# Second block's mixers in one stream of equal steps: every product with hT taken from weights in two parts, eight ring slots lent, gates by tanh

## The reference

```
for l in range(DEPTH):                                    # DEPTH = 2
    x = x + 0.5 * swiglu_ffn(x, ffn1_norm[l], ffn1_wi[l], ffn1_wo[l])
    h = rms_norm_2(x, mix_norm[l])
    (sb_q, sb_k, sb_v, mla_cq, mla_ckv, mla_kr, nsa_q, ck, cv, sk, sv, wk, wv,
     nsa_gate, merge_gate) = jnp.split(h @ w_in[l], offsets, axis=-1)
    o_sb = stick_breaking_attention(sb_q, sb_k, sb_v)     # 8 heads of 64
    o_mla = mla_attention(mla_cq, mla_ckv, mla_kr, ...)   # 8 heads, 64 + 32 wide
    o_nsa = nsa_attention(nsa_q, ck, cv, sk, sv, wk, wv, nsa_gate, ...)
    gates = sigmoid(merge_gate).reshape(B, S, 3, D_MODEL)
    y = gates[:, :, 0] * (o_sb @ proj_sb[l]) + gates[:, :, 1] * (o_mla @ proj_mla[l]) \
        + gates[:, :, 2] * (o_nsa @ proj_nsa[l])
    x = x + y @ w_out[l]
    x = x + 0.5 * swiglu_ffn(x, ffn2_norm[l], ffn2_wi[l], ffn2_wo[l])
```

## Time and profile before

| | us |
|---|---|
| median of 3 runs | 2982.14 |
| the profiled execution | 2984.02 |
| its span | 2982.7 |
| first mixer, norm to w_out's end | about 1566 to 1964 |
| second mixer, the same | about 2372 to 2779 |
| the four feed-forwards | about 202 to 212 each |

### The profile page before, as it was taken

One profiled execution on the slowest core, in us unless ns is written; L12 is line 12 of the kernel. 1 busy time (PEld: TensorE's weight loads), 2 busy tenths in 40 slices (PEclk: granted clock), 3 DMA queues, 4 the chain that ended last, 5 costly groups with the idle time before them and its releaser, 6 DMA issues.

```text
span 2982.7 us, 31836 instructions
## 1 busy us (share of the span) xinstructions
PE 2459.9 (82%) x13622; PEld 1558.7 (52%) x13622; DVE 1093.7 (37%) x1874; ACT 800.0 (27%) x1143; POOL 3.2 (0%) x7
## 2 busy tenths in 40 slices
PE   7877656767877766677999888889999898887999
PEld 5542111113552111116988454579889774545897
DVE  3741000003640000005544435555455543446554
ACT  3230000002520000004433322444344433324443
POOL 0000000000000000000000000000000000000000
PEclk9888899888878888888999898999999998999999
DMA  8769999997459999998653233356655432424562
GB/s 316 256 233 409 409 409 409 409 409 296 155 224 409 409 409 409 409 409 230 183 184 113 58 92 109 124 141 184 186 155 183 156 112 71 142 71 127 149 180 95
DMA packets 397106, 703.68 MB, mean 236 GB/s; under 512 B 17187, under 2 KB 232483, under 8 KB 396838
## 3 DMA queue, kind: packets, MB, share of 16 engines
q1 hardware_dynamic: 396966, 701.65, 66.2%
HBM read 700.56 MB, written 1.05 MB: 235 GB/s over the span
## 4 chain that ended last, share of the span: by engine, by line
PE 59%; DMA 24%; DVE 7%; ACT 4%; SPq 4%; issue 1%; DVEq 0%; ACTq 0%
PE psum L696 57%; DMA ring<-in_moe_w_up 8%; DMA ring<-in_moe_w_gate 8%; DMA ring<-in_moe_w_down 8%; SPq L566 4%; PE psum L700 2%; DVE arena L1833 1%; ACT ring L1396 1%; DVE lent_r L1833 1%; ACT lent_r L1396 1%; DVE arena L1841 1%; DVE arena L1844 1%; DMA ring<-in_ada_w 0%; DMA ring<-in_cmp_wv 0%; DVE arena_r L1833 0%
## 5 line engine op out<-in xcount | busy, mean ns | idle before, releaser
L696 PE MATMUL psum<-ring,arena 128*32 128x512 f32 (+3 forms) x3672 | 685.4, 664 | 287.3 <-DMA ring<-in_moe_w_up 101.8
L696 PE MATMUL psum<-lent_r 128*128 128x256 f32 (+1 forms) x3440 | 637.8, 299 | 14.3 <-DVE lent_r L1833 14.3
L696 PEld LDWEIGHTS psum<-ring,arena 128*32 128x32 f32 (+2 forms) x3672 | 182.7, 129 | 791.7 <-issue 260.3
L696 PEld LDWEIGHTS psum<-lent_r 128*128 128x128 f32 x3440 | 551.6, 195 | 33.9 <-DVE lent_r L1833 12.1
L696 PE MATMUL psum<-arena_r,lent_r 128*128 128x256 f32 (+1 forms) x1888 | 520.4, 317 | 16.5 <-DVE lent_r L1833 9.3
L1833 DVE TENSOR_TENSOR lent_r<-ring,lent_r 128x2048 fp32r<-128x2048 f32 (+1 forms) x158 | 349.3, 2212 | 279.6 <-ACT lent_r L1396 279.5
L696 PEld LDWEIGHTS psum<-arena_r,lent_r 128*128 128x128 f32 x1888 | 368.0, 195 | 40.1 <-DVE lent_r L1833 10.3
L1396 ACT ACTIVATE lent_r<-ring 128x2048 fp32r<-128x2048 f32 (+1 forms) x158 | 289.9, 1839 | 155.2 <-PE psum L696 154.8
L1396 ACT ACTIVATE arena<-psum 128x512 f32<-128x512 f32 (+3 forms) x118 | 57.8, 501 | 1009.5 <-PE psum L696 935.9
L696 PE MATMUL psum<-ring,hT 128*128 128x512 f32 (+1 forms) x576 | 272.3, 609 | 3.8 <-ACT arena L1396 2.8
L696 PE MATMUL psum<-lent_r,arena_r 128*128 128x512 f32 x1056 | 241.6, 390 | 0.3
(11 more groups left out here) (143 smaller groups left out, 1504.0 us busy)
## 6 DMA issues: line engine op xcount, KB each, us to landing
ring<-in_moe_w_gate SPq DMA_DIRECT2D x128, 1024.0 KB, 18.6
ring<-in_moe_w_up SPq DMA_DIRECT2D x128, 1024.0 KB, 18.6
ring<-in_moe_w_down SPq DMA_DIRECT2D x128, 1024.0 KB, 18.7
ring<-in_ffn_wi SPq DMA_DIRECT2D x176, 512.0 KB, 5.1
ring<-in_ada_w SPq DMA_DIRECT2D x48, 1024.0 KB, 7.5
ring<-in_w_in SPq DMA_DIRECT2D x46, 1024.0 KB, 5.1
ring<-in_ffn_wo SPq DMA_DIRECT2D x44, 1024.0 KB, 4.9
ring<-in_w_out SPq DMA_DIRECT2D x8, 1024.0 KB, 4.8
```

The costliest lines, as they stand in the source:

```text
L696: return T.matmul(out, lhsT, rhs, start=start, stop=stop, **kw)
```

## The change

- The plain `hT` is no longer written; its place holds the high part (`hT_r`). All of w_in is cut: the eight groups of `fill_cols` are 16 pieces more, and the NSA gates one of 192 columns. In the mixers the low part is written over the weight in its ring slot (`ring_r`), so the slot is held until its products end (`multiplied`); the high part goes to one of two buffers.
- `lend(MIX_LENT)` lends eight slots, five go round. After w_out's load two come back.
- One generator `main()` on each of PE, ACT and DVE holds 26 pieces (`mi_list`: low, low, f0, f2, sv, sv, f1, f3, f4, gates, 16 fills) in four steps each, and the products of the first two branches with their projections in 16 steps, 120 steps in all. A step on PE is 12 products of 256 columns or 6 of 512. It uses banks 6 and 7 in turn.
- `mixer_start` runs 9 steps, then `mla_prepare` in 5 parts with 6, 3, 3, 2, 2 steps between (MLA_LEAD). A has a step at each turn of a stream, B too, C two (STEPS_C). Before the second half of the compression `far_enough` runs the stream on to step 57, so that keys and values are there.
- MLA's preparation has banks 4 and 5; its seven first copies go from DVE to ACT. NSA attention turns in bank 4 alone and has its output in bank 5.
- The compression's first product has the weight as the stationary operand and gives the turned result; the transpose and DVE's copy after it go.
- sigmoid(z) is 0.5 + 0.5 tanh(z/2): ACT copies the gates out of PSUM with Tanh; DVE's `opened` does (tanh + 1) x product, and the factor 0.5 is in y's parts. Only the third branch is merged after C.

```diff
-STEPS_A = (1, 1, 3)
+MIX_LENT = 8
+SPLIT = (0, 1, 2, 3, 4, 5, 6, 7)
+MLA_LEAD = (6, 3, 3, 2, 2)
+STEPS_A = (1, 1, 2)
-STEPS_C = 1
+STEPS_C = 2
...
+    mi_list = [("low", 0), ("low", 1), ("f", 0), ("f", 2), ("sv", 0), ("sv", 1), ("f", 1), ("f", 3), ("f", 4), ("gates", 0)] + [
+        (n, h) for n in SPLIT for h in range(2)]
...
     def piece(st, c, p, *pieces):
-            load((st, c, p), E.cut_low.at(st, c, p, 1), *pieces)
+            load((st, c, p), multiplied(st, c, p) if st in in_place else E.cut_low.at(st, c, p, 1), *pieces)
...
+            lend(MIX_LENT)
+            for p in range(4):
+                mi(p)
+            load(("uq", layer), ...)
+            mi(4)
+            load(("ukv", layer), ...)
+            for p in range(5, 9):
+                mi(p)
+            piece("mi", layer, mi_list.index(("gates", 0)), cols_chunk(w, C_GATE, 24))
+            fill_loads(layer, 0)
+            fill_loads(layer, 1)
+            compress_loads(layer, 0)
+            fill_loads(layer, 2)
+            compress_loads(layer, 1)
+            for i in range(3, 8):
+                fill_loads(layer, i)
...
+    KV_STEPS = 4 * (mi_list.index((1, 1)) + 1) + 1
+    def mixer_start(fill, mla):
+        for _ in range(9):
+            next(fill)
+        for n in MLA_LEAD:
+            next(mla)
+            for _ in range(n):
+                next(fill)
...
+                for p, (kind, i) in enumerate(mi_list):
+                    T.wait_ge(*E.cut_low.at("mi", l, p, 1 if p else 0))
+                    for j in range(2):
+                        b = 6 + j
...
+                            for k in range(4):
+                                kk = 4 * i + k
...
+                                op = mm3(psum[:, b, 0:width], (high[:, kk, tok], low[:, kk, tok]),
+                                         cut_part("mi", l, p, k * width, width), kk == 0, kk == KT - 1)
+                                if k == 1:
+                                    step()
+                                    yield
...
-            weave(fill, STEPS_C, (attention(nsa_units, 12 + 12 * l, bufs=mx.bufs), 1))
+            weave(fill, STEPS_C, (attention(nsa_units, 12 + 12 * l, turn_banks=(4,), out_bank=5, bufs=mx.bufs), 1))
             run(fill)
-            for br in range(3):
...
+            T.wait_ge(*E.o_low.at(l, 2))
+            for h in range(2):
+                if h:
+                    T.wait_ge(*E.o_low.at(l, 3))
+                rows_piece_product("mo", l, 4 + h, mx.oT_high[2], mx.oT_low[2], 2 * h, 4, [0, 1, 2, 3])
...
+                for p, (kind, i) in enumerate(mi_list):
+                    if p:
+                        second(p - 1)
+                    if p + 1 < n_mi:
+                        cut("mi", l, p + 1)
...
+                    stt(mx.y[:, t, half], mx.merge[:, br, t, half], 1.0, psum[:, bank, :], ALU.add, ALU.mult)
```

More of the change, by code:

```diff
@@ L1793, in mixer @@
-            run(fill)
-            C.preload_act_table(ACT.Sigmoid)
-            cut("mo", l, 0, 0)
-            for br in range(3):
-                if br == 2:
-                    C.wait_ge(*E.o_out.at(12 + 12 * l + 7))
-                af(mx.oT_high[:, br], mx.oT[:, br], ACT.Copy).then_inc(*act.ev(E.o_high, l, br))
-            for br in range(3):
-                af(mx.merge[:, br], mx.merge[:, br], ACT.Sigmoid).then_inc(*act.ev(E.opened, l, br))
-            pieces = cuts("mo", l, 10)
-            for _ in range(6):
-                next(pieces)
+            C.wait_ge(*E.o_out.at(8 + 12 * l + 3))
@@ L1808, in mixer @@
-            run(pieces)
+                af(mx.yT_high[:, k, :], psum[:, 4 + k % 4, 0:S], ACT.Copy, scale=0.5).then_inc(*act.ev(E.yT_high, l, k))
+            cut("mo", l, 8)
+            cut("mo", l, 9)
         C.wait_ge(E.cols_in, 16)
@@ L2497, in mixer, with opened @@
-            for i2, (c0, width) in enumerate(mi_tokens):
-                next(pieces)
-                next(pieces)
-                V.wait_ge(*E.mi_pe.at(l, ("t", 2 * i2 + 1)))
-                dst = (mx.sv, mx.low)[i2][:, 0, :]
-                cp(dst, psum[:, 2 * i2, 0:width]).then_inc(*dve.ev(E.mi_dve, l, ("t", i2)))
+            cut("mi", l, 0, 1)
+            done = [0]
+            def opened(br, b):
+                t, half = b // 2, slice(b % 2 * 512, (b % 2 + 1) * 512)
+                bank = 6 + b % 2 if br < 2 else b
+                V.wait_ge(*E.rows.at("mo", l, 2 * br + 1, b))
+                if br == 0:
+                    stt(mx.y[:, t, half], mx.merge[:, br, t, half], 1.0, psum[:, bank, :], ALU.add, ALU.mult).then_inc(
+                        *dve.ev(E.merged, l, br, b))
+                else:
+                    alone(stt(mx.prod[:, b % 2, :], mx.merge[:, br, t, half], 1.0, psum[:, bank, :], ALU.add, ALU.mult))
+                    tt(mx.y[:, t, half], mx.y[:, t, half], mx.prod[:, b % 2, :], ALU.add).then_inc(*dve.ev(E.merged, l, br, b))
@@ new lines, in mixer @@
+            weave(fill, STEPS_B[0], (attention(mla_units, 8 + 12 * l, [(0, 1)], [2], 3, mx.bufs), STEPS_B[1]), (nsa_all(), STEPS_B[2]))
+            weave(fill, STEPS_C, (attention(nsa_units, 12 + 12 * l, turn_banks=(4,), out_bank=5, bufs=mx.bufs, after=after), 1))
+            run(fill)
+            cut("mo", l, 4)
+            cut("mo", l, 5)
+            o_low(3)
+            for b in range(4):
+                opened(2, b)
+                if b == 1:
+                    cut("mo", l, 6)
+            cut("mo", l, 7)
```

620 lines of the change are left out of this document (357 added, 263 removed).

## The result

The changed kernel takes 3099.07 us (median of 4 runs, 3095.14 to 3099.27) against 2982.76 (2981.45 to 2986.21): a ratio of 1.038, with a 95% interval of 1.037 to 1.040. The forecast was 2902, with a range of 2846 to 2952. The change is slower by 116 us, 58 a mixer. The runs that follow are compared by medians, their stretches by the profiled execution of each.

A forecast was written before the change was run, and what follows sets the result against it. TensorE bound the first products; small waits and low clock added time in stick-breaking (A), MLA (B) and NSA attention (C). Per mixer -6.2 to attention's end, -30.7 after, -3 at the start: -39.9, two -80, 2902 us; range 2846 to 2952.

The forecast's parts named there:

- Fill products: Stick-breaking through NSA attention: plain products taking 132.5 us become products of parts at 88.3, a gain of 44 a mixer.
- Clock: Stick-breaking and MLA attention: of at most 24 us lost to half clock, 5 a mixer are won back.
- The sign that I named for it: Clock forecast is wrong if the granted clock in stick-breaking and MLA attention is below 0.86.
- The ring: Mixers' weight loads: five slots instead of seven add 6 us of TensorE idle time a mixer, range 0 to 16.
- My sign for it: Ring forecast is wrong if TensorE's wait for a DMA at the compression is over 10 us.
- The cuts in the queues: DVE and ACT orders: softmax steps late behind weight cuts cost 3 us a mixer, range 0 to 40.
- Rival 3: Slower: TensorE waits for a 4.2 us cut pair at each of 20 pieces, 84 us a mixer; 3066 us; chance 0.07.
- my own sign, over 1 us a piece: Queue forecast is wrong if TensorE waits for cuts for over 1 us a piece.
- The compression: NSA preparation: keeps its 64 products in other shapes; its transposes and their waits go, -3 us a mixer.
- NSA attention: Summed with stick-breaking and MLA attention as one stretch; 22.1 us of branch products paid in the stream.
- the end: Last attention product to first w_out product: 52.2 us become 21.5, a gain of 30.7 a mixer.
- the waits at the second turn in C: NSA attention, one bank for turning: TensorE waits for ACT about 1.2 us each; 5 us a mixer counted.

The follow-up runs named there:

- e4: Changed kernel with one product instead of three in each fill step, low-part products left out: 3058.6 us.
- e5: Kernel before the change with its plain fill products 384 columns wide instead of 512: 2948.4 us, ratio 0.988.
- e12: Kernel before the change with two fill steps instead of one at each MLA-preparation turn during stick-breaking, compression loads one group later: 2966.6 us, ratio 0.995.
- e6: Changed kernel with seven ring slots instead of five (one shared gate buffer) and cuts of 14 fill pieces shortened to 128 columns: 3024.4 us.
- e9: Changed kernel with seven ring slots, shortened cuts of 14 fill pieces, and the compression's first-product operands as before the change, together: 3010.3 us.
- e1: Changed kernel with seven slots in the mixers' ring instead of five, room coming from one gate buffer shared by three branches: 3055.8 us.
- e3: Changed kernel with cuts of 14 of 16 fill pieces shortened from 2048 to 128 columns on ACT and DVE: 3063.1 us.
- e13b: Changed kernel with cuts shortened to 128 columns for 14 fill pieces and the four pieces of the first two branches: 3051.6 us.
- e7: Changed kernel with the operands of the compression's first product as before the change, the turn of its result left out: 3078.3 us.
- e8: Changed kernel with two more high-part buffers, so the first branch's two pieces are cut beside the last fill; gates shared: 3086.0 us.
- e10: Changed kernel with one product instead of three in three feature pieces (f1, f3, f4) that run during stick-breaking: 3095.3 us.
- e11: Changed kernel with two stream steps instead of one at each MLA-preparation turn during stick-breaking, the stream run on to step 64 there: 3105.0 us.

## Why the prediction was wrong, step by step

- **Fill products, "a gain of 44".** This step failed first. It set 132.5 us, measured at mixed clock, against 88.3 at full clock, so some 18 us of clock were counted as product work before the clock's own term. And it took TensorE's work for time. A is 96 to 98 us in the changed kernel with one product or three; e4 got 20 us a mixer for 59 of products, and even in the kernel before e5 got 17 for 28.5. That A had room could be read before the change (88 us busy at 0.86 in 99), and e12 used it; that it also gives way when work is taken out (98.7 to 90.5 us in the first mixer of e5) could not.
- **Clock, "I take 5 of it".** Wrong in sign: A fell from 0.86 to 0.74, the MLA part from 0.96 to 0.76, NSA attention from 1.00 to 0.91, some 39 us a mixer. The sign that I named for it, A and B below 0.86, is there. In the MLA part the clock followed the waits and the compression's operands, about half each (e6 0.85, e9 0.96). In A it followed the work: at nearly the same length it was 0.86, 0.74 and 0.63 as there was less to do. "It fell where TensorE had been waiting" is not the whole of it: in the changed kernel it fell within the compression's 32-column products with no idle time, and in the kernel before at about 2437.5, 1 us behind 3.65 us of 24-column gate products, when TensorE had been busy for 11.4 of 12 us. The rule that I set aside, the Trainium skill's "TensorE: Matmul & The Clock Gate", section "A second HAM failure mode: psum-queue depth-cycling" (short idles between groups over changing banks make the clock swing), agrees with the rows in so far as idle time grew from 36 to 84 us and the clock fell; no run varied the banks, and the falls without idle time are not of its kind. The row of feed-forward by which I judged it had no idle time at all, so it could not speak for or against.
- **The ring, "6, range 0 to 16".** Measured 22 a mixer (e1), outside its range. The count of TensorE work that covers a landing was right for TensorE, which waited only 4.9 for a load; but ACT waited 24.7, and its queue holds the norms' sqrt behind the cut. My sign for it, a DMA wait of TensorE over 10, stayed silent for that reason. I had asked who waits for the load, not who stands behind the one that waits.
- **The cuts in the queues, "3, range 0 to 40".** About 18 for the fills (e3) and 6 for the branches (e13b, nearly all of it the passage below), inside the range at eight times the value taken. Rival 3 came nearest in time (3066), but in part by luck: it priced cuts alone, at 81 us a mixer over my 3, where they cost 24, and left out ring and clock. It also wanted TensorE's waits to name cuts, and 11.5 of 96 us do; my own sign, over 1 us a piece, stayed silent too (18.6 us with the passage, over 30 pieces).
- **The compression, "its 64 products in other shapes".** Priced at nothing; 10 us a mixer (e7). The products themselves cost the same at equal clock (0.11 us a record), but in the new order the clock fell to half among them.
- **The passage to the first branch.** Not in the sum at all: 7 us a mixer (e8). With two buffers of high parts a cut cannot run ahead of the last fill.
- **NSA attention.** 22 us of branch products were paid in the stream as forecast, but the stretch grew by 48: 234 products of parts (54 us at 0.230) stand there where 32 plain ones (29 us at 0.89) stood, 7 are the passage, the rest short waits and a clock of 0.91. I had summed A to C as one; A took only 21 of the 120 steps, and this stretch, where TensorE had been busy for 49 of 54 us at full clock, took 39, the most.
- **Right:** the end (25 us; 21.5 forecast), the copies at the start (from the last feed-forward product to the mixer's first 7.5 us for 9.6; 3 less forecast), the feed-forwards unchanged, no table loads between tanh and softmax (none in ACT's timeline of NSA attention), the waits at the second turn in C (0.7 each, 1.2 forecast), DVE's and ACT's cut durations.

What stays open: e9 is still 14 us a mixer over the kernel before and some 54 over the forecast. The runs put that on NSA attention and on gains of product work that A and the clock did not give, but they do not part these two to the microsecond; and the shortened cuts and shared gates of e9 are no kernel that computes the reference.

## What to carry to other kernels

Before counting products as time, look at each stretch for busy share times clock: where a chain of small steps sets the length, work taken away can lower the clock and leave the length (e10), and work put in can cost less than it weighs (e12 took 13 us of it in 8, e11 11 in 9). Both have to be tried: the same A gave way in e5. An instruction that waits for a load, put into an in-order queue with a softmax or norm behind it, must be priced by what stands behind it. A waits list names the last link; only the chain shows the load or cut in front of it. And compare two forms of a product at equal clock before calling one of them dear: here the form moved the clock, and the clock took the time.

## What the chip showed unexpectedly

- TensorE's granted clock fell to 0.63 in a stretch in which it was busy for 78 of 97 us (e10), and was 0.98 at 100 of 107 (e12): both with the same attention steps.
- A wait that the profile lists as "issue" (7.06 us) was one for a semaphore: giving the cuts their own buffers removed it.
- 64 records of plain f32 with a stationary weight of 128 x 128 and 32 moving columns, with TensorE busy throughout, ran at a clock of 1.00 for 5.4 us and at 0.51 for the next 3.3; the next 64 took 13.8 us, all at 0.50. With 32 columns standing and 128 moving the first 64 took 7.17 us at 1.00 (kernel before and e7). Time x clock is 7 us for each 64 in all of them.
- Adding 512-column products raised the clock of the stick-breaking stretch from 0.86 to 0.98 (e12).
